# Reciprocals of the softmax sums spread by small transfers through DRAM, and a PSUM bank of its own for each block's last fill group

## What is computed

```python
p, lse = masked_softmax(scores, mask)            # exp(s - lse)
out = einsum('...qk,...ke->...qe', p, vw)         # values weighted by p
```

## Time and profile before

| | |
|---|---|
| median of 3 runs | 2954.13 us |
| profiled execution, whole / span | 2957.55 / 2955.7 us |
| TensorE busy | 2924.0 us, 99% |
| VectorE busy | 1992.6 us, 67% |
| ScalarE busy | 1232.5 us, 42% |
| GpSimd busy | 930.5 us, 31% |
| removed transpose, L3024 | 100, each modelled at 270 ns |
| removed copy, L1482 | 100, 31.8 us busy in all |
| granted TensorE clock | 0.996 of full speed (2.4 GHz) |

### The profile page before, as it was taken

How to read it: one execution, slowest core, us unless ns; L and a number is a source line. 1 busy time by engine, 2 the same in 40 slices (tenths; PEclk the granted TensorE clock), 3 DMA queues, 4 the chain that set the end, 5 groups by cost and what they waited for, 6 DMA issues and landing times.

```text
span 2955.7 us, 50329 instructions
## 1 busy us (share of the span) xinstructions
PE 2924.0 (99%) x19328; PEld 2757.5 (93%) x19328; DVE 1992.6 (67%) x3695; ACT 1232.5 (42%) x2377; POOL 930.5 (31%) x762
## 2 busy tenths in 40 slices
PE   9999999999999999999999999999999999999998
PEld 8888887999999999999988888889999999999998
DVE  7877756388644448687878777563987444476786
ACT  5444544454322225444554444444534222255342
POOL 1211212755522226001442111137556222250013
PEclk9999999999999999999999999999999999999999
DMA  4111031333222225734521110223232222358245
GB/s 163 47 59 54 21 97 65 118 111 122 87 71 70 70 70 189 234 119 156 188 99 54 51 59 22 101 81 132 82 119 80 70 70 70 97 166 270 88 145 199
DMA packets 153451, 307.92 MB, mean 104 GB/s; under 512 B 16128, under 2 KB 76160, under 8 KB 152960
## 3 DMA queue, kind: packets, MB, share of 16 engines
q1 hardware_dynamic: 148784, 292.14, 30.2%
q10 hardware_dynamic: 4432, 12.58, 1.2%
HBM read 239.12 MB, written 57.67 MB: 100 GB/s over the span
## 4 chain that ended last, share of the span: by engine, by line
PE 89%; DVE 6%; issue 2%; POOL 1%; ACT 1%; DMA 1%; SPq 0%; ACTq 0%; DVEq 0%; POOLq 0%
PE PS L2849 27%; PE PS L2851 26%; PE PS L2850 26%; PE PS L3015 3%; PE PS L2999 3%; PE PS L2983 2%; PE PS L2971 1%; PE PS L2887 1%; POOL OSS L1400 1%; DVE ACCUM L2169 0%; PE PS L2943 0%; DVE SW L2462 0%; DVE ACCUM L2161 0%; DVE PT L2594 0%; PE PS L3024 0%
## 5 line engine op out<-in xcount | busy, mean ns | idle before, releaser
L2849 PE MATMUL PS<-XH,WH 128*128 128x512 f32 (+1 forms) x1152 | 432.9, 376 | 7.7 <-DVE VD L2440 2.8
L2851 PE MATMUL PS<-XH,WL 128*128 128x512 f32 (+1 forms) x1152 | 410.2, 356 | 0.0
L2850 PE MATMUL PS<-XL,WH 128*128 128x512 f32 (+1 forms) x1152 | 408.7, 355 | 0.0
L1428 POOL TENSOR_TENSOR GL<-GR,GH 128x512 fp32r<-128x512 f32 x186 | 251.6, 1365 | 366.4 <-ACT GH L1795 304.5
L2849 PE MATMUL PS<-DHH,DWH 128*128 128x384 f32 (+1 forms) x1056 | 328.3, 311 | 0.0
L2851 PE MATMUL PS<-DHH,DWL 128*128 128x384 f32 (+1 forms) x1056 | 326.6, 309 | 0.0
L2850 PE MATMUL PS<-DHL,DWH 128*128 128x384 f32 (+1 forms) x1056 | 325.8, 309 | 0.0
L2849 PEld LDWEIGHTS PS<-XH,WH 128*128 128x128 f32 x1152 | 217.8, 189 | 64.7 <-issue 27.1
L2851 PEld LDWEIGHTS PS<-XH,WL 128*128 128x128 f32 x1152 | 217.7, 189 | 32.7
L2850 PEld LDWEIGHTS PS<-XL,WH 128*128 128x128 f32 x1152 | 218.5, 190 | 24.5
L2850 PE MATMUL PS<-CL0T,GH 128*128 128x384 f32 x704 | 238.4, 339 | 0.0
(11 more groups left out here) (270 smaller groups left out, 8278.6 us busy)
## 6 DMA issues: line engine op xcount, KB each, us to landing
GR<-w_gu SPq DMA_DIRECT2D x62, 768.0 KB, 4.2
RAW<-w_in SPq DMA_DIRECT2D x48, 512.0 KB, 3.7
DHR<-hidden SPq DMA_DIRECT2D x66, 320.0 KB, 4.5
DWR<-w_down SPq DMA_DIRECT2D x66, 256.0 KB, 3.9
S3B<-w_down SPq DMA_DIRECT2D x66, 256.0 KB, 3.3
GR<-w_gu SPq DMA_DIRECT2D x62, 256.0 KB, 2.8
T3B<-hidden SPq DMA_DIRECT2D x44, 320.0 KB, 4.0
hidden<-S1T SPq DMA_DIRECT2D x44, 192.0 KB, 1.9
```

Source lines behind the costliest of these rows:

```text
L1428: nc.gpsimd.tensor_tensor(GL[v % 2][:, m, :, :], GR[v % 2][:, m, :, :], GH[v % 2][:, m, :, :].bitcast(F32), ALU.subtract).then_inc(s_wlo_r ...
L2849: nc.tensor.matmul(out, wh, xh, start=first, stop=False, skip_group_check=reopened)
L2850: nc.tensor.matmul(out, wh, xl, start=False, stop=False, skip_group_check=reopened)
L2851: return nc.tensor.matmul(out, wl, xh, start=False, stop=last, skip_group_check=reopened)
```

## The change

The 100 transposes of L3024 and the 100 copies of L1482 are gone, with their semaphores. In their place ACT stores the two columns of reciprocals of a pair to a small DRAM tensor `rates` (`send_rates`, two transfers of 128 x 4 bytes, directly after `across` of the same pair) and one unit later loads each back as one row repeated on 64 partitions (`fetch_rates`, two transfers of 64 x 512 bytes, ahead of that unit's copies). `fetch_rates` waits until both stores have landed. `y` waits for the loads and multiplies two tiles in SBUF; on VectorE it moves from the head of the odd unit to behind the reciprocal of that unit. `across` of a pair now waits until `y` of the one before is done (YS is read by it), and the values matmuls wait only for `s_summed`. The last pair's `fetch_rates`, `y` and block store move into the next block: the fetch after the first part of `split_v`, `y` behind the masks of units 0 and 1, `store_block` and `second_biases` to the start of unit 1. In the last block of a layer the last fetch and `y` follow at once.

The last fill group of blocks 0 to 3 goes to bank 1 (`CLOSING_BANK`), one of the banks of the even units' scores, which units 16 and later don't use. It waits for the mask of unit 15 in place of the drain of the group before it, and `turn_v` of the next block, which also writes bank 1, waits for its drain.

```diff
+def closing(kind, i, c):
+
+    return any((kind, i) == FILL[b][-1] and c == last_chunk((kind, i)) for b in range(LAST))
...
-            def spread_inverse(pair):
-
-                pool.wait_ge(s_inverse, pair + 1)
-                if pair:
-                    pool.wait_ge(s_rb, pair)
-                a = 2 * (pair % 2)
-                nc.gpsimd.tensor_copy(RC[:, :, :], SM[:, a:a + 2].unsqueeze(2).to_broadcast([P, 2, HD])) \
-                    .then_inc(s_recip, 1)
...
-                        if u % 2:
-                            spread_inverse(NP * (BLOCKS * L + b) + u // 2)
...
+            def send_rates(done):
+
+                a = 2 * (done % 2)
+                act.wait_ge(s_inverse, done + 1)
+                for h in range(2):
+                    act.dma_start(rates[done % 2, h, :].unsqueeze(1), SM[:, a + h:a + h + 1]).then_inc(s_rate_out, 16)
+
+            def fetch_rates(done):
+
+                act.wait_ge(s_rate_out, 32 * (done + 1))
+                for h in range(2):
+                    act.dma_start(RATE[done // NP % BLOCKS not in DIL][h][0:HD, :],
+                                  rates[done % 2, h, :].unsqueeze(0).to_broadcast([HD, P])).then_inc(s_rate_in, 16)
...
+                    act.wait_ge(s_yb, 2 * (NP * nb + pair))
...
+                if b:
+                    fetch_rates(NP * nb - 1)
                 exp(0)
                 split_v(nb, slice(4, None))
                 for u in range(NU):
+                    if b and u == 1:
+                        store_block(L, b - 1)
+                        if b - 1 == DIL[-1]:
+                            second_biases(L)
+                    if u > 1 and u % 2:
+                        fetch_rates(NP * nb + u // 2 - 1)
                     if u and u % 2 == 0:
                         across(u // 2 - 1)
+                        send_rates(NP * nb + u // 2 - 1)
...
+                send_rates(NP * nb + NP - 1)
+                if b == LAST:
+                    fetch_rates(NP * nb + NP - 1)
...
-                    if b != LAST:
-                        store_block(L, b)
-                    if b == DIL[-1]:
-                        second_biases(L)
...
+            def y(L, b, pair):
+
+                done, i = NP * (BLOCKS * L + b) + pair, units_of(b)[2 * pair][0]
+                if pair == 0 and b:
+                    dve.wait_ge(s_yout, 16 * (4 * L + b))
+                dve.wait_ge(s_summed, 2 * (done + 1))
+                dve.wait_ge(s_rate_in, 32 * (done + 1))
+                for h in range(2):
+                    own = slice(HD * h, HD * h + HD)
+                    rate, total = RATE[b not in DIL][h][0:HD, :], YS[0:HD, h, :]
+                    if b not in DIL and i < 8:
+                        to = queries(YB, i)
+                        rate, total = (t.rearrange("p (r c) -> p r c", c=Q_COLS) for t in (rate, total))
+                    else:
+                        to = stepped(YB, *half_of(i)) if b in DIL and i < 8 else YB[:, i * P:(i + 1) * P]
+                    nc.vector.tensor_tensor(to[own], rate, total, ALU.mult).then_inc(s_yb, 1)
...
-                    if u > 1 and u % 2:
-                        y(u // 2 - 1)
...
+                if b:
+                    y(L, b - 1, NP - 1)
...
                         nc.vector.reciprocal(SM[:, a:a + 2], SM[:, a:a + 2]).then_inc(s_inverse, 1)
+                    if u > 1 and u % 2:
+                        y(L, b, u // 2 - 1)
...
-                        pe.wait_ge(s_yb, 2 * (NP * nb + pair))
+                        pe.wait_ge(s_summed, 2 * (NP * nb + pair))
...
-                def spread_recip(pair):
-
-                    pe.wait_ge(s_recip, NP * nb + pair + 1)
-                    pe.wait_ge(s_summed, 2 * (NP * nb + pair + 1))
-                    nc.tensor.transpose(PS[:, Y_BANK, 0:P], RC[:, :, :].rearrange("p h d -> p (h d)"), ident) \
-                        .then_inc(s_rb, 1)
...
+                        if closing(*key[1:]):
+                            pe.wait_ge(s_masked, first + 2 * NP - 4)
+                        else:
+                            drained(fill_groups(L, b)[before - 1] if before else holder)
...
+                if b:
+                    drained(fill_groups(L, b - 1)[-1])
                 turn_v(nb, slice(0, 4))
...
+        if closing(kind, i, c):
+            return CLOSING_BANK
```

More of the change, by code:

```diff
@@ L66 @@
 FILL_BANK = 7
+CLOSING_BANK = 1
 Y_BANK = 6
@@ L498, in build @@
 def build(nc, xt, w_in, w_out, w_gu, w_down, gains, conv_w, bias, tables, small, mixed,
-          parked, hidden, out):
+          parked, hidden, rates, out):
     with ExitStack() as ctx:
@@ L569, in build @@
         YS = place("YS", [P, 2, P], offset=base + 97984)
-        RC = place("RC", [P, 2, HD], offset=base + 99008)
+        RATE = [[place(f"RATE{n}{h}", [P, P], offset=o) for h, o in enumerate(pair)] for n, pair in
+                enumerate(((base + 99008, base + 97376), (w_at + 4 * 8192 + 3072, w_at + 4 * 8192 + 3584)))]
         MH = [place(f"MH{c}", [P, KT, n], F32R, offset=SCRATCH + KT * t0 * 4) for c, (t0, n) in enumerate(OCHUNKS)]
@@ L678, in build @@
         s_inverse = sem("inverse")
-        s_recip = sem("recip")
+        s_rate_out = sem("rate_out")
+        s_rate_in = sem("rate_in")
         s_across = sem("across")
         s_summed = sem("summed")
-        s_rb = sem("rb")
         s_yb = sem("yb")
@@ L2562, in add_parts @@
                         .then_inc(s_summed, 1)
[L2564 to L2569, removed]
-                    dve.wait_ge(s_rb, NP * nb + pair + 1)
-                    for h in range(2):
-                        own = slice(HD * h, HD * h + HD)
-                        if b not in DIL and i < 8:
-                            rate, total = (t.rearrange("p (r c) -> p r c", c=Q_COLS)
-                                           for t in (PS[own, Y_BANK, 0:P], YS[0:HD, h, :]))
-                            nc.vector.tensor_tensor(queries(YB, i)[own, :, :], rate, total, ALU.mult).then_inc(s_yb, 1)
-                            continue
-                        to = stepped(YB, *half_of(i)) if b in DIL and i < 8 else YB[:, i * P:(i + 1) * P]
-                        nc.vector.tensor_tensor(to[own, :], PS[own, Y_BANK, 0:P], YS[0:HD, h, :],
-                                                ALU.mult).then_inc(s_yb, 1)
                 mask(0)
                 mask(1)
+                if b:
+                    y(L, b - 1, NP - 1)
                 drain(*last_cover)
@@ L2603, in attention @@
                         nc.vector.reciprocal(SM[:, a:a + 2], SM[:, a:a + 2]).then_inc(s_inverse, 1)
+                    if u > 1 and u % 2:
+                        y(L, b, u // 2 - 1)
                     with_unit(u)
                 add_parts(NP - 1)
-                y(NP - 1)
+                if b == LAST:
+                    y(L, b, NP - 1)
             def dil_table(i, h, nkt):
@@ L3035, in fill @@
                         before = fill_groups(L, b).index(key)
-                        drained(fill_groups(L, b)[before - 1] if before else holder)
+                        if closing(*key[1:]):
+                            pe.wait_ge(s_masked, first + 2 * NP - 4)
+                        else:
+                            drained(fill_groups(L, b)[before - 1] if before else holder)
                         pe.wait_ge(s_lo, SPLIT[key[:3]])
@@ L3046, in attention @@
                 if b not in DIL:
-                    pe.wait_ge(s_yb, 2 * NP * nb)
+                    pe.wait_ge(s_summed, 2 * NP * nb)
                     turn_v(nb, slice(4, None))
@@ L3058, in attention @@
                         output_group(L, 0, 0, range(2) if u == NU - 3 else range(2, 4))
-                    if u and u % 2 == 0:
-                        spread_recip(u // 2 - 1)
                 if b != LAST:
@@ L3069, in attention @@
                     output_group(L, 0, 0, range(4, KT))
-                spread_recip(NP - 1)
             def output_group(L, c, i, ts):
@@ L3324 @@
     hidden = nc.dram_tensor("hidden", [FT, P, T], F32, kind="Internal").ap()
+    rates = nc.dram_tensor("rates", [2, 2, P], F32, kind="Internal").ap()
     out = nc.dram_tensor("out", [P, KT, T], F32, kind="ExternalOutput").ap()
-    build(nc, *args, mixed, parked, hidden, out)
+    build(nc, *args, mixed, parked, hidden, rates, out)
     r = run_bass_kernel_spmd(nc, [arrays], core_ids=[0])
```

## The result

The changed kernel takes 3557.93 us (median of 4 runs, 3551.68 to 3562.37) and the kernel before, on the same chip, 2954.88: a ratio of 1.2031, 95% interval 1.2016 to 1.2046. It is 20% slower; I had forecast 2962 us and a range up to 2998. The direction was right, the size was off by some 600 us.

The account below looks back on a forecast made before the run. TensorE, busy in 99% of the span, was taken as the bound. Terms -15.8 + 10.6 + 2.4 + 9 + 2 = +8.2 us on the profiled 2957.55 gave about 2966; the median being 3.4 lower, 2962 us, range 2943 to 2998.

Parts of the forecast that it names:

- stalls above the gain: The forecast's own case for the whole kernel: stalls somewhat larger than the gain, 2962 us, chance 0.4.
- The loop: From across through stores, loads and y to the next across, once a pair: 5.8 us, bounds 5.1 to 8.5.
- S: Landing time of a pair's small stores of reciprocals: taken as 2.05 us, bounds 1.5 to 3.4.
- R: Landing time of the loads that spread the reciprocals: taken as 2.05 us, bounds 1.9 to 3.4.
- The rival of slow stores: Small stores land after 3.4 us, loads after 2.05; loop 7.15, 42 us of stalls, 2991 us; chance 0.2.
- both at 3.4: Stores and loads each land after 3.4 us: loop 8.5, 52 us a layer, time 3053 us.
- What the loop holds up: TensorE waits where across to across is shorter than the loop, in each layer's last two blocks: 10.6 us in all.
- The end of a layer, nothing: ACT is held 3.5 us from 528.40; its next copy feeds a group opened some 8 us later: no cost.
- 100 transposes at 0.11 and the waits, -15.8: Gain on TensorE: 11.0 us for removed transposes, 2.8 for waits on VD, 2.0 for waits on low parts.
- The copy behind across at A+0.95 instead of A+0.40: With across starting at A, two store issues delay ACT's copy of probabilities; TensorE stalls about 0.3 us in narrow pairs.
- Moved biases, 4.5 a layer: Block store and bias tables at unit 1 of block 3 hold ACT and the first small store: 9 us, bounds 3 to 14.
- VD's waits: TensorE's four waits on VectorE's drain into VD at block ends vanish with the new bank: 2.8 us gained.

Follow-up runs that it names:

- the padded kernel: The changed kernel with each reciprocal stored to its own 512 B row of DRAM and the loads reading constants: 3034.71 us, 1.0255.
- the run in which nobody waits: The changed kernel storing a constant column, stores awaited only two pairs later, loads reading constants once reciprocals are known: 3222.99 us, 1.0895.
- the run with the operand in PSUM: The changed kernel without its four transfers per pair, biases, y and block store at old places, y's first operand read from PSUM: 2944.3 us, 0.9956.
- the bank alone: The kernel before with only the closing group's new bank, reciprocals as before: 2953.99 us, 0.9994.

## Why the prediction was wrong

By ratios, the 20.3% come to this: packed addresses of the stores 17.8 (of it the clock's share and up to 3 for the slower loads), landing and issue of good stores 1.5, loads 0.9, moved biases 0.25, the place of `y` and `y`'s operand in SBUF together 0.4, less a gain of 0.44. The direction was right by the mechanism that I had named, stalls above the gain; but I had given slower only 0.5, and the forecast was 8 us from no change.

- **The loop, 1.7 + S + R, with S = R = 2.05.** The failed step is the size of S, the landing of the small stores. S was 7.4 to 9.8 us alone and 7.3 to 12.2 from send to fetch in the kernel (17.5 and 18.0 at the ends of the layers), four times the value and over twice my upper bound of 3.4. The rival of slow stores named the right place and a price that was still too low; "both at 3.4", 3053 us, was my worst case. (At a loop of 7.15 blocks 0 to 2 lose 0.3 us a layer by their times, not the 1.2 that I wrote; the 42 us should have been 40.) The bound came from rows of loads and wide stores, none of which has several partitions write into the same 32 B, and a row of another kind bounds nothing from above. R was 2.4 alone and 2.5 in the padded kernel, but 3.4 in the changed one, at my upper bound. The path was right: with S down to 1.5, in the padded kernel, the shortest loop is 5.7 us where I had 5.8, and blocks 0 to 2 lose nothing.
- **What the loop holds up.** I counted the loop against the across-to-across times and put 10.6 us on the last two blocks. With S that large, blocks 0 to 2 stall too (42 to 54 us each), as I had written under what would refute me. The share of ACT's order is separate: without the wait in ACT's queue (the run in which nobody waits) 335 us of the 600 are gone.
- **The end of a layer, nothing.** I took 3.5 us for ACT's hold and let the copy behind it be late for free. The last stores took 17.5 and 18.0 us, and TensorE waited 27.2 us for the weights behind them. Even with good stores it is 6.6 us, in the padded kernel.
- **S as one number.** Even at my price the sum was too small: the padded kernel has a median of 1.9 from send to fetch, less than the 2.5 that I took, and loses 77 us against before, not 8; its stores and loads cost some 70 us where I had 15. Blocks 3 and 4 hold 64 of the 77 us. In up to 33 of all pairs the stores land late, and in the ones that I followed SyncE's loads or ACT's own larger transfers were in flight; I held the small transfers against their own bytes only. That these collisions make up the larger part of the stores' 44 us is read from the rows and wasn't isolated.
- **The clock.** None of my terms had it. TensorE's work took 97.6 us more in the first attention stage at 0.83 granted. In the padded kernel, with shorter stalls, the first 275 us of that stage are at 1.00 and the last 110 us at 0.92.
- **100 transposes at 0.11 and the waits, -15.8.** Right as a price (13 us, by the run with the operand in PSUM), but not had in full: I costed `y` "behind the reciprocal" and never its operand's new home. That GpSimd works beside it stood in the profile of before.
- **The copy behind across at A+0.95 instead of A+0.40.** Right, a little high: 0.86 to 0.92 in most pairs of the kernel after (698.35 against 697.47). The issues: 0.81 us for two stores as taken, but 1.10 for two loads where I had 0.33 to 0.45 each.
- **Moved biases, 4.5 a layer.** 3.5 by the run that moves them back, in a kernel without the small stores, so this is ACT's hold alone, which I had at 1.4. The other part, the first small store behind them in the queue, shows in the padded kernel: 7.7 and 7.0 us from send to fetch against 1.9, and a first pair of block 3 that is 7.6 and 5.4 us longer where I had 4 to 5. The mechanism was right and the price too low.
- **VD's waits.** Gone as forecast with the bank alone, 2.8 us in a list; in time at most 0.15%, not told from nothing. In the changed kernel 2.7 us of them remain.

## What to carry to other kernels

Before a small transfer goes into a loop that must close in every unit, measure it alone with its own addresses: packed 4-byte writes from 128 partitions into DRAM took 7.4 to 9.8 us, the same writes 32 B apart 1.43. A transfer that ScalarE waits for holds all its work behind the wait, and its landing here was a distribution (1.9 us in the median, up to 7.9 in the padded kernel) and not a number. Ask of every such wait what stands behind it at the ends of the stages too. When an operand moves from PSUM to SBUF, look at what GpSimd does at that time.

## What was not expected of the hardware

- 128 writes of 4 B to DRAM: 7.4 to 9.8 us at a step of 4 B, 3.0 to 3.9 at 8 B, 1.5 to 2.2 at 16 B, 1.42 to 1.43 from 32 B to 1 KB.
- Loads issued 1 us behind two such stores in the same queue landed 8.4 us after their issue instead of 3.1 (medians, to the instruction that waited). The weights' loads on SyncE's queue were late as well, 7.0 us in the kernel after and 6.7 with nobody waiting, against 3.7 before.
- Two fp32 multiplications of 64 x 128 took 3.20 us beside a GpSimd operation of 2.45 with both inputs in SBUF, and 0.80 with one in PSUM.
- ACT issues two loads of a repeated row in 1.10 to 1.12 us, against 0.81 for two stores.
